# Two transformer layers on one core: operands of the split matmuls at other places modulo 256 bytes

## The reference

```
first block:
  h = rmsnorm(x);  proj = h @ w_in                      # 3080 columns
  y = [forgetting attention, 8 heads of 64 | chunked attention, 8 heads of 64]
  x = x + rmsnorm(y @ w_out)
  q = rmsnorm(x) @ w_mq;  k, v = rmsnorm(mem) @ w_mk, rmsnorm(mem) @ w_mv      # 256 memory rows
  x = x + rmsnorm(attention(q, k, v) @ w_mo)
  x = x + rmsnorm(square(relu(rmsnorm(x) @ w_ff1)) @ w_ff2)                    # inner width 4096
second block:
  proj = rmsnorm(x) @ w_in_2                            # 8280 columns
  gated delta rule (8 heads of 128) and sparse attention with a top-64 index, gated and merged
  x = x + merged @ w_out_2
  x = x + square(relu(rmsnorm(x) @ w_mlp_up_2)) @ w_mlp_down_2                 # inner width 4096
```

## The kernel before

| tensor | before | after |
|---|---|---|
| `w_raw`, `w_lo`, `w_hi` (all slots) | 128 | 128 |
| `h_hi`, `h_lo` | 128 | 0 |
| `hid_hi`, `hid_lo`, `hid_r`, `hid_v`, first feed-forward | 64 | 96 |
| the same, second feed-forward | 64 | 160 |
| `m_hi`, `m_lo` | 64 | 160 |
| `x`, `xn`, `cst` (holds the identity of the transposes) | 128 | 128 |
| attention and delta-rule buffers (`mqT`, `mkT`, `mv`, `PT`, ...) | 64 | 64 |

## Time and profile before

### The profile page before, as it was taken

One profiled execution on the slowest core, in us unless ns is written; L12 is line 12 of the kernel. 1 busy time (PEld: TensorE's weight loads), 2 busy tenths in 40 slices (PEclk: granted clock), 3 DMA queues, 4 the chain that ended last, 5 costly groups with the idle time before them and its releaser, 6 DMA issues.

```text
span 920.1 us, 14611 instructions
## 1 busy us (share of the span) xinstructions
PE 897.4 (98%) x5672; PEld 797.0 (87%) x5672; DVE 575.2 (63%) x899; ACT 511.8 (56%) x932; POOL 89.6 (10%) x111
## 2 busy tenths in 40 slices
PE   6999999999999999999999999999999999999998
PEld 6998977888899998887778989988899799998886
DVE  5455656664676664445656998889846676665333
ACT  4466666664665554335557668787255465554330
POOL 0010000000000000001000412241152101000000
PEclk9999999999999999999999999999999999999999
DMA  9756333464455566555364544454430456555552
GB/s 341 254 183 230 107 124 108 148 226 92 146 175 184 183 207 185 195 202 195 107 214 138 184 139 141 134 164 157 99 143 1 131 190 184 184 183 183 184 189 84
DMA packets 110395, 152.22 MB, mean 165 GB/s; under 512 B 6752, under 2 KB 68344, under 8 KB 109944
## 3 DMA queue, kind: packets, MB, share of 16 engines
q1 hardware_dynamic: 110328, 151.31, 50.7%
HBM read 147.99 MB, written 3.30 MB: 164 GB/s over the span
## 4 chain that ended last, share of the span: by engine, by line
issue 48%; PE 34%; DVE 9%; ACT 4%; POOL 2%; DVEq 1%; DMA 1%; POOLq 1%; ACTq 0%; SPq 0%
PE acc L455 4%; PE acc L469 4%; PE acc L467 4%; PE acc L468 4%; PE acc L457 4%; PE acc L456 4%; DVE s_w_lo L405 3%; ACT s_w_hi L399 1%; PE acc L495 1%; DVE s_qkvT L1522 1%; PE acc L497 1%; PE acc L496 1%; DMA s_w_raw<-in_w_out 1%; ACT s_relu_i L1445 1%; POOL s_rstd L636 1%
## 5 line engine op out<-in xcount | busy, mean ns | idle before, releaser
L405 DVE TENSOR_TENSOR s_w_lo<-s_w_raw,s_w_hi 128x2048 fp32r<-128x2048 f32 (+1 forms) x198 | 312.2, 1594 | 176.5 <-ACT s_w_hi L399 176.2
L399 ACT ACTIVATE s_w_hi<-s_w_raw 128x2048 fp32r<-128x2048 f32 (+1 forms) x198 | 262.7, 1345 | 148.6 <-PE acc L457 102.3
L467 PE MATMUL acc<-s_h_hi,s_w_hi 128*128 128x256 f32 x800 | 229.1, 286 | 0.8 <-DVE s_h_lo L690 0.8
L469 PE MATMUL acc<-s_h_hi,s_w_lo 128*128 128x256 f32 x800 | 227.3, 284 | 0.0
L468 PE MATMUL acc<-s_h_lo,s_w_hi 128*128 128x256 f32 x800 | 227.3, 284 | 0.0
L467 PEld LDWEIGHTS acc<-s_h_hi,s_w_hi 128*128 128x128 f32 x800 | 154.5, 193 | 1.6 <-issue 1.2
L468 PEld LDWEIGHTS acc<-s_h_lo,s_w_hi 128*128 128x128 f32 x800 | 154.6, 193 | 0.3
L469 PEld LDWEIGHTS acc<-s_h_hi,s_w_lo 128*128 128x128 f32 x800 | 154.4, 193 | 0.0
L457 PE MATMUL acc<-s_w_hi,s_hid_lo 128*128 128x512 f32 x224 | 88.3, 394 | 0.0
L456 PE MATMUL acc<-s_w_lo,s_hid_hi 128*128 128x512 f32 x224 | 87.8, 392 | 0.0
L455 PE MATMUL acc<-s_w_hi,s_hid_hi 128*128 128x512 f32 x224 | 86.9, 388 | 0.0
(11 more groups left out here) (323 smaller groups left out, 1429.1 us busy)
## 6 DMA issues: line engine op xcount, KB each, us to landing
s_w_raw<-in_w_in SPq DMA_DIRECT2D x43, 1024.0 KB, 5.2
s_w_raw<-in_w_ff SPq DMA_DIRECT2D x32, 1024.0 KB, 5.2
s_w_raw<-in_w_mlp_up SPq DMA_DIRECT2D x16, 1024.0 KB, 5.5
s_w_raw<-in_w_mlp_down SPq DMA_DIRECT2D x16, 1024.0 KB, 5.0
s_w_raw<-in_w_out SPq DMA_DIRECT2D x8, 1024.0 KB, 5.1
s_w_raw<-in_w_mk SPq DMA_DIRECT2D x4, 1024.0 KB, 5.4
s_w_raw<-in_w_mv SPq DMA_DIRECT2D x4, 1024.0 KB, 5.0
s_w_raw<-in_w_mq SPq DMA_DIRECT2D x4, 1024.0 KB, 5.0
```

What stands on the lines that cost most here:

```text
L399: act.activation(w_hi[u % SPLIT_SLOTS][:, cs], w_raw[u % RAW_SLOTS][:, cs], ACT.Copy).then_inc(w_hi_done, 4 if q is None else 1)
L405: dve.tensor_tensor(w_lo[u % RAW_SLOTS][:, cs], w_raw[u % RAW_SLOTS][:, cs], w_hi[u % SPLIT_SLOTS][:, cs].bitcast(F32), ALU.subtract).then ...
L467: pe.matmul(o, wh[:, cs], hi[:, k, :], start=k == 0, stop=False)
L469: i = pe.matmul(o, wl[:, cs], hi[:, k, :], start=False, stop=k == KC - 1)
```

## The change

It puts 128 unused bytes ahead of `h_hi` and 128 behind `h_lo`, so that `h` moves by 128 bytes and everything behind it by 256, which leaves the places modulo 256 of the rest as they were. It puts 96 bytes ahead of `m_hi`. It gives each feed-forward its own four tensors for the inner activations, behind 32 unused bytes for the first and 96 for the second; they take the same room one after the other, and the functions of the feed-forward take them from `HID[tag]`. No instruction is added, removed or moved on any engine, no wait changes, and all shapes stay.

```diff
         w_hi = [sb(f"w_hi{i}", [P, 2048], F32R) for i in range(SPLIT_SLOTS)]
+        sb("before_h", [P, 32])
         h_hi = sb("h_hi", [P, KC, S], F32R)
         h_lo = sb("h_lo", [P, KC, S], F32R)
+        sb("behind_h", [P, 32])
         x = sb("x", [P, NT, D])
...
         mv = sb("mv", [P, NT, D], at=r1)
+        sb("before_m", [P, 24], at=r1)
         m_hi = sb("m_hi", [P, KC, S], F32R, at=r1)
         m_lo = sb("m_lo", [P, KC, S], F32R, at=r1)
         r1.close()
 
-        r2 = ExitStack()
-        hid_hi = sb("hid_hi", [P, FF // P, S], F32R, at=r2)
-        hid_lo = sb("hid_lo", [P, FF // P, S], F32R, at=r2)
-        hid_r = sb("hid_r", [P, 2, 512], at=r2)
-        hid_v = sb("hid_v", [P, 2, 512], at=r2)
-        r2.close()
+        def hidden_buffers(tag, floats):
+
+            at = ExitStack()
+            if floats:
+                sb("before_" + tag, [P, floats], at=at)
+            bufs = [sb(tag + "_hi", [P, FF // P, S], F32R, at=at), sb(tag + "_lo", [P, FF // P, S], F32R, at=at),
+                    sb(tag + "_r", [P, 2, 512], at=at), sb(tag + "_v", [P, 2, 512], at=at)]
+            at.close()
+            return bufs
+
+        HID = {"ff1": hidden_buffers("hid", 8), "up": hidden_buffers("hid2", 24)}
...
-            act.activation(hid_r[:, j % 2, :], hid_bank(tag, j)[:], ACT.Relu).then_inc(relu_done, 1)
+            act.activation(HID[tag][2][:, j % 2, :], hid_bank(tag, j)[:], ACT.Relu).then_inc(relu_done, 1)
...
             def hidden_mm(tag):
+                hid_hi, hid_lo = HID["ff1" if tag == "ff2" else "up"][0:2]
```

More of the change, by code:

```diff
@@ L1088, in hid_dve_sq @@
             b = units[of[tag][j]]["banks"][0] if j >= NT else units[of[tag][0]]["banks"][j]
-            dve.scalar_tensor_tensor(hid_v[:, j % 2, :], hid_bank(tag, j)[:], 0.0, hid_r[:, j % 2, :], ALU.max, ALU.mult).then_inc(acc_free[b], 1)
+            dve.scalar_tensor_tensor(HID[tag][3][:, j % 2, :], hid_bank(tag, j)[:], 0.0, HID[tag][2][:, j % 2, :], ALU.max, ALU.mult).then_inc(acc_free[b], 1)
         def hid_tr_pe(pe, tag):
@@ L1096, in hid_tr_pe @@
                 for c in range(4):
-                    i = pe.transpose(aux[t][:, c * P:(c + 1) * P], hid_v[:, t, c * P:(c + 1) * P], ident())
+                    i = pe.transpose(aux[t][:, c * P:(c + 1) * P], HID[tag][3][:, t, c * P:(c + 1) * P], ident())
                 i.then_inc(hid_tr, 1)
@@ L1102, in hid_act_hi @@
                 N.wait(act, hid_tr)
-                act.activation(hid_hi[:, 0:4, j * P:(j + 1) * P], aux[j][:].rearrange("p (c s) -> p c s", c=4), ACT.Copy).then_inc(hid_hi_done, 1)
+                act.activation(HID[tag][0][:, 0:4, j * P:(j + 1) * P], aux[j][:].rearrange("p (c s) -> p c s", c=4), ACT.Copy).then_inc(hid_hi_done, 1)
             else:
                 wait_read(act, of[tag][j])
-                act.activation(hid_hi[:, 2 * j:2 * j + 2, :], hid_v[:, j % 2, :], ACT.Copy).then_inc(hid_hi_done, 1)
+                act.activation(HID[tag][0][:, 2 * j:2 * j + 2, :], HID[tag][3][:, j % 2, :], ACT.Copy).then_inc(hid_hi_done, 1)
         def hid_dve_lo(dve, tag, j):
@@ L1111, in hid_dve_lo @@
                 ts = slice(j * P, (j + 1) * P)
-                dve.tensor_tensor(hid_lo[:, 0:4, ts], aux[j][:].rearrange("p (c s) -> p c s", c=4), hid_hi[:, 0:4, ts].bitcast(F32),
+                dve.tensor_tensor(HID[tag][1][:, 0:4, ts], aux[j][:].rearrange("p (c s) -> p c s", c=4), HID[tag][0][:, 0:4, ts].bitcast(F32),
                                   ALU.subtract).then_inc(hid_lo_done, 1)
             else:
-                dve.tensor_tensor(hid_lo[:, 2 * j:2 * j + 2, :], hid_v[:, j % 2, :], hid_hi[:, 2 * j:2 * j + 2, :].bitcast(F32),
+                dve.tensor_tensor(HID[tag][1][:, 2 * j:2 * j + 2, :], HID[tag][3][:, j % 2, :], HID[tag][0][:, 2 * j:2 * j + 2, :].bitcast(F32),
                                   ALU.subtract).then_inc(hid_lo_done, 1)
```

## The result

The changed kernel takes 927.99 us (median of 4 runs, 927.68 to 928.21) where the kernel before takes 922.12 us beside it (4 runs, 921.76 to 922.33). The ratio is 1.0062, 95% interval [1.0048, 1.0076]: slower, by 5.9 us. The forecast was 908.3 us, faster. In a comparison, runs are of the same state of the chip.

What follows compares the result with a forecast made beforehand. PE's step from matmul to matmul was taken as the bound. Gains of 12.7 + 0.9 = 13.6 us took the 920.1 us span to 906.5, plus 1.8 for the median: 908.3 us; range 899 to 922 us.

Steps and rivals of the forecast that it cites:

- "no effect" rival: Whole kernel: placement is worth nothing, the memory's shorter step comes from its company in the attentions; 921.9 us, chance 0.06.
- Form B with `h`, 15.6 us: 2400 matmuls, 256 `h` columns moving past stationary weights: step from 120.0 to 113.5 ns, 15.6 us, of which 12.7 arrive.
- rows 7: Trace rows of narrow projections; with 8 columns, three steps take 0.34 us at distance 128, 0.35 at the same place.
- the one of 88 columns: Projection with stationary chunks at 32 and 160, cited as a mixed witness: 22 steps in 2.59 us, 117.7 ns each.
- Form A with `h`, 0 us with ends of 2.3: 1008 matmuls, 512 weight columns moving past stationary `h`: step stays 226.7 ns, 0 us, ends 2.3 us either side.
- Form A with `hid`, 0.9 us gained: 768 matmuls, weights moving past stationary `hid`: middle of 229.0 and 226.7 ns, 1.15 ns each; ends 1.8 us gained or lost.
- The memory: 0, end 1.2 us: 192 matmuls with moving `m`, from 64 to 160: no change from 113.5 ns; at the end 6.5 ns each lost.
- The 2.9 us taken off form B: Gains not reaching the end: 1.4 us before DVE's maximum, 1.0 in sparse attention, 0.2 at the start, 0.3 elsewhere.
- More than I take: Rival: fast streams lose all excess, steps of 109 ns (256 columns) and 216 ns (512); 879.6 us, chance 0.08.
- Slower: form A collides: Rival: loading the stationary activation meets the 512 moving weight columns longer, 236 ns, 14.8 us lost; 924.0 us, chance 0.08.
- point of decision: Extra step at which 1776 matmuls of 512 columns cancel the 12.7 us gain: 7.2 ns each.

Runs made afterwards that it cites:

- runs 5 and 6: One program, run twice: against the kernel before, `h` moved from 128 to 64 and both `hid` from 64 to 128; 911.64 us, then 909.33 us with more runs.
- run 4: Against the kernel before, only `h` moved, to 64 (distance -64 from the weights at 128); 917.72 us, ratio 0.9955.
- run 3: All operands of the split matmuls 64 bytes further than in the kernel before, so the distances stay; 922.28 us, ratio 1.0003.

## Why the prediction was wrong

**What bounds it: held.** PE was the limit, no instruction moved, and the steps explain the 5.8 us. The "no effect" rival, which the Trainium skill's two rules spoke for ("SBUF — State Buffer", section "SBUF: two separate sides", and "TensorE: Matmul & The Clock Gate", section "Step-by-step: what each phase is for"), falls: runs 5 and 6 differ from the kernel before in unused bytes only, and take 0.990 and 0.988 of its time. (The memory's pieces, whose company it held responsible, have 24 matmuls in the timeline, not 12.) The two rules name nothing that depends on the distance of two addresses; the measurement decides.

**Form B with `h`, 15.6 us: the step that failed first.** It took the 113.5 ns of the memory, which stands at distance -64, for distance 128, "since rows 7 at distance 128 come to the same". They did not: run 4 shows 113.5 ns with `h` at -64, and at 128 form B takes 118.8 to 120.1 ns. The term was 0.0 us in one feed-forward and 0.8 in the other where 4.1 each was forecast. The witness could not bear the weight: 0.34 against 0.35 us over three steps is one unit of the timeline's last digit, 3.3 ns a step, as much as the difference read from it (the trace's nanoseconds have 340 and 347, 2.3 ns a step), and its stationary operand had 8 columns, not 128. The forecast preferred the witness that agreed over the one of 88 columns (117.7 ns), which came nearer.

**Form A with `h`, 0 us with ends of 2.3: the step that failed in size and sign.** It was 233.3 ns in `w_mo`, 6.6 ns more, and 4.0 ns more on the mean of all its steps. That 226.7/512 equals 113.5/256 was read as an undisturbed pace, so that a move could do no harm; it showed only that the kernel before already stood at the best of form A's distances tried here. The ends were the difference of two known distances, which bounds nothing at a third.

**Form A with `hid`, 0.9 us gained: wrong in sign.** Of -32 and +32 only the first lies between -64 and 0, and the step doesn't lie between theirs at either: 233.3 ns at both, 228.9 and 226.7 at the two known. Lost were 3.4 us, the largest term of the result. The middle of two points was taken of a quantity that was not known to be monotonic.

**The memory: 0, end 1.2 us.** The keys went to 116.5 ns, 192 x 3.0 = 0.6 us; inside the end.

**What hides it.** The 2.9 us taken off form B, mostly for DVE's waits, never came into play, since PE arrived later, not earlier. The writes of ACT and DVE at new places cost nothing in run 3, as forecast.

**The rivals.** "More than I take" falls: no run came under 113.4 and 226.7 ns. By its sentence on the Trainium skill ("Back-to-back issue gap") the steps would be 109.2 and 215.8 ns. That section gives the formula for an isolated matmul, and for a stream with weight loads a lower figure, about 131 ns at 512 columns; this case's streams, 226.7 ns at best, agree with neither. "Slower: form A collides" had the outcome: it put 1776 matmuls of 512 columns at 236 ns against form B's gain. The step is 233.3 ns with `hid`, 768 x 4.4 = 3.4 us, and 232 to 235 ns with `h`, where the trace's sum is 3.9 us more. That a load collides with the moving stream, the reason that the rival gave, no run shows. Its point of decision was put at 7.2 ns "or from less if form B gains less", and form B gained only some 2 us (the sum over its steps in the trace). The prediction named it and gave it 0.08, on the ground that the two known places differ by 2.3 ns only. With three distances new to form A and none of them in the trace, that was far too little.

## What to carry to other kernels

Where PE runs split fp32r matmuls without a gap, the distance modulo 256 bytes between the two operands in SBUF was worth 1 to 2% of the time here (909.3 us at best, 928.0 at worst), and the form decides which distance is good: 0 for 512 moving weight columns, -64 for 256 moving tokens. Measure the distances on the chip before placing anything. A step known at one distance says nothing of another, even between two known ones. And if part of a kernel sits at its best distance already, a common move of one operand pays there what it gains elsewhere: give each form its own place.

## What the runs showed of the hardware that was not expected

- The step follows the distance and not the places: with 64 bytes more for every split operand the three rows of the first feed-forward fell within 0.01 us of those before, up to 432 us (run 3). The exception is form B at -64, where the places seem to have a say in which of two paces comes.
- In form A all distances but 0 (226.7 ns) and -64 (228.9) cost 233.3 or 234.3 ns, and the sign counts. In form B's feed-forwards distance 0 is at the slow end (120.1, as 128 in some stretches) and -64 has the best step (113.5); +32, +96 and -96 were not tried there.
- At distance -64 form B has two paces, 113.5 and 117.9 ns, and at 128 also two, 118.8 and 120.1. One lasts through a stage of 624 matmuls, and the other can hold in the next stage of the same execution. What chooses is open: with `h` at 64 and the weights at 128 both paces have filled feed-forwards, with `h` at 128 and the weights at 192 only the slower one has, in the two programs traced. The total of one program scatters accordingly, from 908.7 to 919.0 us where the kernel before scatters from 921.5 to 924.1.
- Why a distance costs anything, bank or port or otherwise, no run here tells.
